# Six single-row loads in place of three paired loads for the old rows of a windowed key and value cache

## The reference

```
x = x + 1/2 * SwiGLU_1(RMSNorm(x))
q, k, v, a, g = split(RMSNorm(x) @ W_in)
x = x + [windowed attention(q, k, v) | convolution branch(a, g)] @ W_out
x = x + cross attention(RMSNorm(x), memory)
x = x + 1/2 * SwiGLU_2(RMSNorm(x));   final RMSNorm
```

## Time and profile before

| | |
|---|---|
| median of 3 runs | 2822.71 us (2821.54 to 2823.26) |
| profiled execution, own time | 2822.71 us |
| its span, first to last instruction | 2820.9 us |
| mean granted TensorE clock | 0.969 of full speed |
| TensorE busy | 2615.2 us, 93% |
| sample attention | from about 1340 to 1495 us of the span |

### The profile page before, as it was taken

How to read it: one execution, slowest core, us unless ns; L and a number is a source line. 1 busy time by engine, 2 the same in 40 slices (tenths; PEclk the granted TensorE clock), 3 DMA queues, 4 the chain that set the end, 5 groups by cost and what they waited for, 6 DMA issues and landing times.

```text
span 2820.9 us, 43430 instructions
## 1 busy us (share of the span) xinstructions
PE 2615.2 (93%) x16775; PEld 2462.6 (87%) x16775; DVE 1093.6 (39%) x2017; ACT 548.9 (19%) x1303; POOL 697.1 (25%) x404
## 2 busy tenths in 40 slices
PE   7999999999998999688998898769799999999998
PEld 6899999999997999566556897649799999999998
DVE  5223333233335799333433523533633233333234
ACT  4200000000002233265222212321200000000002
POOL 6522222222221222022001210102222222222220
PEclk9999999999999999899998999989899999999999
DMA  7311111111110122243863113651111111111101
GB/s 214 120 45 45 45 45 45 45 45 40 42 41 26 30 68 77 94 137 124 324 237 97 43 47 114 246 182 46 45 45 45 45 45 39 43 42 40 45 30 64
DMA packets 208166, 224.93 MB, mean 80 GB/s; under 512 B 10938, under 2 KB 180982, under 8 KB 203987
## 3 DMA queue, kind: packets, MB, share of 16 engines
q1 hardware_dynamic: 191031, 195.58, 21.3%
q10 hardware_dynamic: 17052, 28.21, 2.7%
HBM read 191.10 MB, written 32.67 MB: 79 GB/s over the span
## 4 chain that ended last, share of the span: by engine, by line
PE 83%; DVE 7%; issue 4%; DMA 3%; ACT 2%; PEld 1%; POOL 1%; SPq 0%; DVEq 0%; ACTq 0%; PEldq 0%; POOLq 0%
PE ps L694 24%; PE ps L696 23%; PE ps L695 23%; PE ps L1084 1%; PE ps L1128 1%; DVE ps L1908 1%; PE ps L1098 1%; DVE hidl L1812 1%; PE ps L1011 1%; PE ps L1022 1%; PE ps L994 1%; DVE hl L1885 1%; PE ps L1232 1%; DMA cK<-in_cache_mem_k 1%; PE ps L1177 1%
## 5 line engine op out<-in xcount | busy, mean ns | idle before, releaser
L694 PE MATMUL ps<-hh,wh 128*128 128x384 f32 (+1 forms) x3168 | 1042.2, 329 | 62.3 <-DVE hl L1854 26.1
L695 PE MATMUL ps<-hh,wl 128*128 128x384 f32 (+1 forms) x3168 | 1039.7, 328 | 0.0
L696 PE MATMUL ps<-hl,wh 128*128 128x384 f32 (+1 forms) x3168 | 1039.6, 328 | 0.0
L694 PEld LDWEIGHTS ps<-hh,wh 128*128 128x128 f32 x3168 | 600.9, 190 | 66.3 <-issue 57.7
L695 PEld LDWEIGHTS ps<-hh,wl 128*128 128x128 f32 x3168 | 600.7, 190 | 0.3
L696 PEld LDWEIGHTS ps<-hl,wh 128*128 128x128 f32 x3168 | 600.5, 190 | 0.0
L636 POOL CAST wh<-raw 128x1024 fp32r<-128x1024 f32 x148 | 154.6, 1045 | 1469.4 <-PE ps L696 1340.8
L1824 DVE TENSOR_TENSOR ht<-ps,sg 128x384 f32<-128x384 f32 x132 | 70.6, 536 | 927.8 <-PE ps L696 926.4
L638 POOL TENSOR_TENSOR wl<-raw,wh 128x1024 fp32r<-128x1024 f32 x148 | 367.5, 2483 | 11.9
L694 PE MATMUL ps<-hidh,bh 128*128 128x384 f32 (+1 forms) x1056 | 346.7, 328 | 11.7 <-DVE x L1836 11.7
L1836 DVE SCALAR_TENSOR_TENSOR x<-ps,x 128x384 f32<-128x384 f32 (+1 forms) x528 | 276.5, 533 | 185.5 <-PE ps L696 184.9
(11 more groups left out here) (243 smaller groups left out, 2068.3 us busy)
## 6 DMA issues: line engine op xcount, KB each, us to landing
raw<-in_ffn_gate SPq DMA_DIRECT2D x44, 512.0 KB, 3.8
raw<-in_ffn_up SPq DMA_DIRECT2D x44, 512.0 KB, 3.8
raw<-in_ffn_down SPq DMA_DIRECT2D x44, 512.0 KB, 3.5
Kw<-in_cache_win_k SPq DMA_DIRECT2D x24, 512.0 KB, 5.7
Vw<-in_cache_win_v SPq DMA_DIRECT2D x24, 512.0 KB
raw<-in_w_in SPq DMA_DIRECT2D x20, 512.0 KB, 3.7
Kw<-in_cache_win_k SPq DMA_DIRECT2D x8, 1024.0 KB, 8.2
Vw<-in_cache_win_v SPq DMA_DIRECT2D x8, 1024.0 KB
```

The costliest lines, as they stand in the source:

```text
L694: pe.matmul(out, w_hi_, a_hi, start=first, stop=False)
L695: pe.matmul(out, w_lo_, a_hi, start=False, stop=False)
L696: return pe.matmul(out, w_hi_, a_lo, start=False, stop=last)
```

## The change

The old rows are loaded by six DMAs in place of three. Each covers 16 groups of 16 rows, and each of 128 partitions gets one row (2 KB) into one block. The same 768 rows are read, and 256 KB instead of 512 KB by each DMA. Which row stands at which partition and block differs, so the bias is built for the new order. `KD` and `VD` grow by 48. The loads of the recent rows and of `Vn`, and the work of all the other engines, are the same.

```diff
@@ sample_bias
-    block = np.arange(OB)[:, None]
-    old = block // 2 * (4 * P) + (part // 4 * 16 + part % 4 * 2)[None, :] + block % 2
+    old = np.arange(OB)[:, None] * (2 * P) + (part // 8 * 16 + part % 8)[None, :]
@@ decoder_layer
-    KD = (OB // 2 + 1) * 16
-    VD = (OB // 2 + 2) * 16
+    KD = (OB + 1) * 16
+    VD = (OB + 2) * 16
@@ load_rows
-            old = c[0:OLD, :].rearrange("(n g s r) e -> n g s (r e)", g=32, s=8, r=2)
-            for n_ in range(OB // 2):
-                sp.dma_start(dst[:, 2 * n_:2 * n_ + 2, :], old[n_, :, 0:4]).then_inc(done, 16)
+            old = c[0:OLD, :].rearrange("(n g s) e -> g s n e", g=16, s=16)[:, 0:8]
+            for n_ in range(OB):
+                sp.dma_start(dst[:, n_, :], old[:, :, n_]).then_inc(done, 16)
```

## The result

The changed kernel took 2842.72 us (2837.52 to 2845.28, 4 runs) against 2822.12 us (2817.11 to 2823.26, 4 runs) for the kernel before: ratio 1.0063, 95% interval 1.0043 to 1.0084. It is slower by 0.6%, some 18 to 21 us, and outside my range of 2821.3 to 2826.5. The profiled execution shown here took 2831.94 us with a span of 2830.1 us. It is one of the mild ones; 13 recorded executions of the same kernel took 2828.23 to 2845.28 us.

What follows compares the result with a forecast made beforehand. TensorE, busy 93% of the span, was taken as the bound, with the cache loads hidden. The profiled 2822.7 us plus a stall of 0, plus 0.2 for K2's landing interval, gave 2822.9 us, range 2821.3 to 2826.5.

Steps and rivals of the forecast that it cites:

- Moving the data: DMA engines, old rows of one load: 4.1 to 4.8 us for 1.57 MB, so 0 to 0.7 us more, 0.35 taken.
- Bias and semaphore targets: Bias size and VectorE adds unchanged, TensorE still one wait instruction per sequence with higher targets: cost 0 each.
- Issuing: SyncE: 0.73 us per DMA, 4.4 us for six, so recent rows go out 2.2 us later, beside TensorE's work.
- Count of DMAs and how issue and data combine: Old-row loads: later issue mostly shortens recent rows' standing in line, so landings move about 0.5 us; stall 0.
- the stall of 0 to 2.8 us: TensorE waiting on late K2 and K6: 0 expected, 2.8 us at most; chance 0.80.
- Margins: Time from each load's landing to TensorE's first use: K2 0.7 us, K6 2.3, K1 at least 3.2, V3 7.
- The clock: TensorE's granted clock would hardly react to a stall of 1 to 2 us; no visible cost.
- latency in series: DMA path behind SyncE: three more DMAs at 2.5 us each, some 19 us late, about 2841 us; chance 0.05.
- the Trainium skill's figures: Each DMA 2.0 us plus bytes at 436 GB/s, taken one after another: estimated 6.0 us more per load.
- The full queue on SyncE: SyncE held 4.3 us while issuing K2 and K6: 6.6 us late, 2829.3 us; chance 0.03.
- fewer GB/s while the DMA engines are busy than 325: Sign of a wrong forecast in the profile after: DMA rate while busy below the whole-span 325 GB/s.

Runs made afterwards that it cites:

- e1: Kernel before, still three 512 KB old-row DMAs, but a partition's two rows go to separate blocks, making 2 KB pieces: ratio 0.9999, 2820.48 us.
- e8: Kernel before, still three DMAs of 4 KB pieces, but each as 16 runs of 8 partitions instead of 32 of 4: ratio 1.0084, 2842.41 us.
- e7: Changed kernel with its six DMAs of 2 KB pieces as 32 runs of 4 partitions, 16 KB apart: ratio 1.0004, 2821.55 us.
- e13: Changed kernel with its six DMAs of 2 KB pieces as 64 runs of 2 partitions, 8 KB apart: ratio 1.001, 2823.06 us.
- e2: Kernel before with six 256 KB old-row DMAs of 2 KB pieces in place of three, keeping 32 runs to a DMA: ratio 1.0013, 2822.95 us.
- e9: The changed kernel itself, nothing altered, run again on another chip against the kernel before: ratio 1.0045, 2830.54 us.
- e11: Kernel before with only its old value rows loaded as 16 runs of 8 partitions, keys as before: ratio 1.0005.
- e4: Kernel before with six 256 KB old-row DMAs of 4 KB pieces, each into 64 partitions as 16 runs: ratio 1.0055, 2834.55 us.
- e14: Kernel before with six 256 KB old-row DMAs of 4 KB pieces, each into 64 partitions as 32 runs of 2: ratio 1.0087, 2845.51 us.
- e6: Changed kernel with its 16 runs of 8 partitions 64 KB apart instead of 32 KB: ratio 1.0088, 2843.99 us.
- e12: Changed kernel, 16 by 8 kept, but each set of 8 partitions reads rows from groups 64 KB apart: ratio 1.0048, 2833.8 us.

## Why the prediction was wrong

The step that failed is "Moving the data". I put the piece size alone into it and took the rates of the earlier trace rows as its bounds: 383 and 325 GB/s, 0 to 0.7 us more for 1.57 MB. The changed kernel moved everything in the stage at 280 GB/s while busy. What the pieces cost by themselves is in e1: 369 against 382 GB/s, which fits the bounds. What I hadn't costed was an edit that the diff shows plainly: 32 runs of 4 partitions became 16 runs of 8. I read the two `rearrange` patterns for their addresses and sizes, and not for how the 128 partitions are shared out. e8 makes this edit alone and has the whole slowdown; e7 and e13 have a finer split, and their intervals take in no change. Nor did half of the DMA engines do the work alone: the share is a mean over 16, and it was 84 to 97% in the slow kernels.

The other steps, by the runs:

- Bias and semaphore targets at 0: no run speaks against it. e1 and e2, which change the one or the other, are within 0.13%.
- Issuing: forecast 0.73 us for each DMA and 4.4 for six. After, the six of K2 and the step to the next took 1361.43 - 1356.67 = 4.76 us, the other key loads in the stage 3.8 to 4.9. Right within 0.6 us.
- Count of DMAs and how issue and data combine: e2 (+0.13%, a wait of 0.2 us) bears out the stall of 0 to 2.8 us. As an estimate of six DMAs in place of three it was right; the kernel that it described was e2, not the changed one.
- Margins: K2 was named as the tightest (0.7 us) and is the one that stalls. K6, with 2.3 us, was in time in this execution. V3, with a bound of 7 us, was late. The bounds beyond K2 and K6 took the longest landing of recent rows before, 9.5 us, and that time rests on gaps between the loads in which the DMA engines caught up. The change took the gaps away, and the longest landing became 18.1 us.
- The clock: I wrote that it would hardly react. A wait of 4.4 us cost 2.4 us more through it. Waits of 1.8 us before cost nothing that shows. In between, the length of the wait doesn't settle it: 3.0 us in e9 left the granted clock at 1.00, 2.0 us in e11 were followed by 0.55. So this term was put at nothing on thin ground even for a stall within the forecast 2.8 us, and for the real one it was wrong.
- The rivals: latency in series would have given about 2841 us, close to the 2842.72 measured. It is nevertheless not what happened: e2 has the same six DMAs and 1.0013. By the Trainium skill's figures I had K1, K2 and K6 "some 11 us late"; the terms are 2.8, 5.3 and 3.7, which is 11.8. The full queue on SyncE didn't appear either; the issues stayed at 0.54 us in the median (longest 1.28). None of my rivals held the true cause, the rate at which the engines move bytes, though the text named "fewer GB/s while the DMA engines are busy than 325" as a sign of being wrong, and this is the line that showed it.

The Trainium skill's rule of large DMAs ("DMA: Bandwidth & Descriptors", section "Bandwidth") pointed the right way, for another reason than the true one: halving the size cost 0.1% here (e2). A better page of the Trainium skill was "SBUF — State Buffer", section "Door 1: The DMA port swizzle". It says that the partitions are reached by 16 ports in a fixed pattern (0 to 3 share one with 32 to 35, and so on), and that partitions 0 to 63 reach only 8 of them. e4 and e14 agree with the second point: 274 and 248 GB/s over the stage against 382. The Trainium skill's "DMA: Bandwidth & Descriptors", section "The descriptor swizzle", adds that in a plain 128-partition transfer each engine's eight descriptors go to the partitions of one such port. If in a 16 by 8 split an engine is bound to 8 neighbouring partitions instead, it writes two ports, and another engine wants the same two. This would explain e6, e8 and e12 against e7 and e13, if the splits 32 by 4 and 64 by 2 are dealt out otherwise than in such blocks of 8. No run here shows which engine writes which partition, so it stays an inference. Shown is that the split decides, that the source orders tried here (runs 32 KB and 64 KB apart, and e12's) don't, and that a target of 64 partitions gives the same picture. Whether the cause of the last is the same isn't shown either.

The size stays partly open. The same kernel lost 0.63% in one set of runs and 0.45% in another, and its profiled execution only some 10 us. A stall begins where the small margin of K2 is used up, and sometimes draws the clock with it, so small differences in the DMA rate (280 and 292 GB/s in the two profiled executions) come out enlarged. How many loads were late in the slower executions of the changed kernel, those around its median of 2842.72 us, no profile here shows; e8, whose profiled execution took as long, had four.

## What to carry to other kernels

Read a change of a DMA's access pattern for how it shares out the partitions, not only for bytes, pieces and count: 128 partitions as 64 by 2 or 32 by 4 ran at 362 to 382 GB/s here, as 16 by 8 or in halves of 64 partitions at 248 to 292 (rates of all the stage's traffic, recent rows included, while the engines are busy). Coarser splits weren't run. When no wait ends on a DMA, also ask how far the loads are from being late, and treat their landing times as valid only as long as the queue runs empty between them. Four loads, with margins that I had put at 0.7 to 7 us, were late together in e8 through one slower rate, and the slow clock after the stalls came to half as much again (2.4 us on 4.4 in the changed kernel, 7.7 on 15.4 in e8).

## What I had not expected of the hardware

- The split of the destination alone, with the same bytes, pieces and count of DMAs, changed the stage's rate from 382 GB/s (before) to 260 (e8).
- Cutting 4 KB pieces to 2 KB was nearly free: 369 GB/s against 382, time ratio 0.9999 (e1).
- The recent rows, whose own DMA was never changed, came later too (11.8 us from issue against 9.4 for K2): a badly split load holds up the ones behind it. Their packets themselves took 414 ns in the median instead of 309.
- After 4.4 us of idleness TensorE ran 2.7 us at a granted clock of 0.50 and 3 us more at 0.63 on the mean.
